# Attention of a decoder layer: one loop over heads, and an unrolled order over head pairs

## The reference, cut to what matters

```python
# MLA, 8 heads, query and key width 96, value width 64, dense causal
s = einsum('bqhd,bkhd->bhqk', qi, k) * scale
p = masked_softmax(s, kpos <= qpos)
o = einsum('bhqk,bkhd->bqhd', p, v)
# NSA, 8 heads in 2 groups that share keys and values, width 64; three branches with a relative bias
#   compressed: 63 keys; selected: all causal 64-token blocks that top-16 of 16 gives; window: the last 512 keys
out = gi[..., 0:1] * o_cmp + gi[..., 1:2] * o_slc + gi[..., 2:3] * o_win
```

## Time and profile before

| what | us |
|---|---|
| median of 3 runs | 4298.7 (4294.97 to 4320.84) |
| the profiled execution | 4301.82 |
| its span | 4300.0 |
| TensorE busy over the span | 3597.1 (84%) |
| VectorE busy | 1310.4 (30%) |
| ScalarE busy | 648.4 (15%) |
| mean granted TensorE clock | 0.822 |

### The profile page before, as it was taken

One profiled execution on the slowest core, in us unless ns is written; L12 is line 12 of the kernel. 1 busy time (PEld: TensorE's weight loads), 2 busy tenths in 40 slices (PEclk: granted clock), 3 DMA queues, 4 the chain that ended last, 5 costly groups with the idle time before them and its releaser, 6 DMA issues. The chain is left out here.

```text
span 4300.0 us, 50598 instructions
## 1 busy us (share of the span) xinstructions
PE 3597.1 (84%) x16004; PEld 2660.0 (62%) x16005; DVE 1310.4 (30%) x3711; ACT 648.4 (15%) x1506; POOL 176.3 (4%) x187
## 2 busy tenths in 40 slices
PE   3447765899999998798499999999999999999970
PEld 1124445667666666465477776877778777777750
DVE  1114551443443343355222221222222222222213
ACT  0001110232333332132101000100011000100100
POOL 0000000000000000011000000000000000000000
PEclk7678885555566655897699999999999999999995
DMA  3222223211111011221566445764677655555716
GB/s 105 94 107 42 44 35 59 48 36 36 36 35 36 23 36 30 95 62 35 199 229 220 172 155 186 261 227 172 224 261 264 220 191 207 214 175 184 263 61 234
DMA packets 345115, 571.32 MB, mean 133 GB/s; under 512 B 123134, under 2 KB 150142, under 8 KB 343912
## 3 DMA queue, kind: packets, MB, share of 16 engines
q1 hardware_dynamic: 304984, 526.53, 36.7%
q0 software_dynamic: 21152, 38.50, 2.6%
q10 hardware_dynamic: 18832, 4.33, 0.5%
HBM read 531.15 MB, written 72.19 MB: 140 GB/s over the span
## 5 line engine op out<-in xcount | busy, mean ns | idle before, releaser
L1539 PE MATMUL ps<-xT_e,wg 128*128 128x128 f32 (+2 forms) x8192 | 1266.8, 318 | 71.1 <-DVE aT L1502 50.0
L1539 PEld LDWEIGHTS ps<-xT_e,wg 128*128 128x128 f32 x8192 | 1224.9, 200 | 126.3 <-DVE aT L1502 54.0
L1550 PE MATMUL ps<-wd,aT 128*128 128x512 f32 x1504 | 650.8, 592 | 0.0
L1550 PEld LDWEIGHTS ps<-wd,aT 128*128 128x128 f32 x1504 | 283.3, 190 | 344.4 <-issue 344.4
L1495 DVE TENSOR_SCALAR gg<-ps,bias 128x128 f32<-128x128 f32 (+2 forms) x256 | 101.4, 396 | 764.5 <-PE ps L1539 764.5
L696 PE MATMUL ps<-kn,qn 64*128 64x512 f32 (+3 forms) x384 | 270.8, 841 | 0.0
L711 PE MATMUL ps<-ident_t,sc 128*128 128x128 f32 x880 | 224.5, 393 | 44.8 <-ACT sc L754 29.4
L1508 DVE COPY ys_e<-ps 128x1024 f32<-128x1024 f32 x47 | 56.1, 1221 | 671.7 <-PE ps L1550 671.7
L754 ACT ACTIVATE sc<-sc,nm 128x640 f32<-128x640 f32 (+15 forms) x256 | 164.3, 642 | 638.2 <-DVE nm L790 638.2
L711 PEld LDWEIGHTS ps<-ident_t,sc 128*128 128x128 f32 x880 | 148.4, 197 | 170.1 <-issue 166.5
L728 PEld LDWEIGHTS ps<-vn,pT 128*128 128x128 f32 x1056 | 233.5, 325 | 0.0
(11 more groups left out here) (284 smaller groups left out, 2891.8 us busy)
## 6 DMA issues: line engine op xcount, KB each, us to landing
wg<-in_w_gate_up SPq DMA_DIRECT2D x128, 2048.0 KB, 7.8
wd<-in_w_down SPq DMA_DIRECT2D x128, 1024.0 KB, 4.9
yr<-d_ys SPq DMA_DIRECT2D x8, 2048.0 KB, 7.3
skew<-d_rev SPq DMA_DIRECT2D x18, 512.0 KB, 5.2
w_in<-in_w_in SPq DMA_DIRECT2D x1, 6880.0 KB
d_strip<-strip SPq DMA_DIRECT2D x9, 512.0 KB, 2.6
x_a<-in_x POOLq DMA_DIRECT2D x8, 512.0 KB, 7.5
kn<-d_kn SPq DMA_DIRECT2D x8, 512.0 KB
```

Of the source, the lines that this page charges most:

```text
L1539: mm = pe.matmul(ps[:, j % 2, half * PASS:half * PASS + w], wg[:, j // 2, k, c0:c0 + 255:2], xT[:, k, 0:w], start=(k == 0), stop=(k == KD ...
L1550: mm = pe.matmul(ps[:, 2 + 2 * b + h, :], aT[:, j, b * P:(b + 1) * P], wd[:, c, j % 2, h * 512:(h + 1) * 512], start=(j == 0), stop=(j == ...
```

## The change

`stage_attend` is written out for pairs of heads, with no loop. A unit is a pair, a branch and a query block. 18 wide units and 14 narrow ones alternate, with m, s and w mixed, and the four last wide ones follow one another.

- The scores of the two NSA heads of a unit are formed from operands in partitions 0 to 63 and 64 to 127, into different banks. They are cut into pieces of at most 512 keys. m keeps 96 rows for each of its heads.
- VectorE's custom instruction now multiplies by -1 and takes the minimum, which gives the negative maximum itself. It is issued for each head and piece, and the second piece starts from the first one's result. L790 goes.
- ScalarE copies the transposed tiles of the first head of the pair, VectorE those of the second.
- The reciprocal, the gate product and some last products are issued once for both heads.
- Loads are double-buffered by pair, and the first two pairs' loads are issued at the start. `sc` is set to zero by GpSimd, over 8192 columns instead of 4096.
- The gates are stored as rows of 24 numbers, and not as 12-byte pieces, and are loaded once, as the last load of the first pair; VectorE waits for them in its second unit.

```diff
-                        with nc.allow_non_contiguous_dma("12-byte gates"):
-                            sp.dma_start(e.d_gt[:, rows, :].rearrange("h p d -> p h d"), gt[b][:, :].rearrange("p (h d) -> p h d", d=3)).then_inc(s_st, 16)
+                        sp.dma_start(e.d_gt[rows, :], gt[b][:, :]).then_inc(s_st, 16)
...
+    BIG = [("m", 7), ("m", 6), ("s", 7), ("m", 5), ("s", 6), ("m", 4), ("w", 7), ("s", 5), ("m", 3), ("w", 6), ("s", 4), ("w", 5), ("m", 2),
+           ("s", 3), ("w", 4), ("s", 2), ("w", 3), ("w", 2)]
+    SMALL = [("m", 1), ("m", 0), ("c", 7), ("c", 6), ("c", 5), ("c", 4), ("c", 3), ("s", 1), ("c", 2), ("w", 1), ("c", 1), ("s", 0), ("c", 0), ("w", 0)]
+    ORDER = [x for i in range(len(BIG)) for x in BIG[i:i + 1] + SMALL[i:i + 1]]
+    PAIRS = HM // 2
+    NU = len(ORDER)
+    UNITS = [(hp, b, q) for hp in range(PAIRS) for b, q in ORDER]
...
+        qm, km = sb("qm", [QK, 2, 2, S]), sb("km", [QK, 2, 2, S])
+        vm = sb("vm", [P, 2, 2, NT, VD])
+        qn = sb("qn", [P, 2, S])
+        kn = sb("kn", [P, 2, 2, S])
...
+        sc = sb("sc", [P, DEPTH, 2, S])
+        pT = sb("pT", [P, 2, 2, S])
+        nm, rs, co = sb("nm", [P, DEPTH, 2, 2]), sb("rs", [P, DEPTH, 2]), sb("co", [P, DEPTH, 2])
...
+        def pieces(u):
+            full = width(*UNITS[u][1:])
+            return [(FIRST[u] + c // 512, c, min(512, full - c)) for c in range(0, full, 512)]
+        def by_scalar(h, g):
+            return h == 0
...
+                pool.memset(sc[:, :, :, :], 0.0).then_inc(s_set, 1)
...
+                def load_mla(hp):
+                    k = hp % 2
+                    if hp >= 2:
+                        sp.wait_ge(s_y, NU * (hp - 1))
+                    sp.dma_start(qm[:, k, :, :], e.d_qm[2 * hp:2 * hp + 2].rearrange("h d n -> d h n")).then_inc(s_lm[k], 16)
+                    sp.dma_start(km[:, k, :, :], e.d_km[2 * hp:2 * hp + 2].rearrange("h d n -> d h n")).then_inc(s_lm[k], 16)
+                    for h in range(2):
+                        sp.dma_start(vm[:, k, h, :, :], e.d_vm[2 * hp + h].rearrange("(t p) d -> p t d", p=P)).then_inc(s_lm[k], 16)
+                def load_nsa(hp):
+                    k, g = hp % 2, hp // 2
+                    sp.dma_start(qn[:, k, :], e.d_qn_flat[2 * hp:2 * hp + 2].rearrange("h d n -> (h d) n")).then_inc(s_ln[k], 16)
+                    for h in range(2):
+                        half = slice(h * HD, (h + 1) * HD)
+                        sp.dma_start(kn[half, k, :, :], e.d_kn[:, g * HD:(g + 1) * HD, :].rearrange("w d n -> d w n")).then_inc(s_ln[k], 16)
+                        sp.dma_start(ck[half, k, :], e.d_ck[g]).then_inc(s_ln[k], 16)
+                        sp.dma_start(strip[:, k, h, :], e.d_strip[2 * hp + h]).then_inc(s_ln[k], 16)
+                        sp.dma_start(wstrip[:, k, h, :], e.d_wstrip[2 * hp + h]).then_inc(s_ln[k], 16)
+                        sp.dma_start(vn[:, k, h, :, :], e.d_vn[h][g].rearrange("(t p) d -> p t d", p=P)).then_inc(s_ln[k], 16)
+                    sp.dma_start(cv[:, k, :], e.d_cv[g]).then_inc(s_ln[k], 16)
+                    if hp == 0:
+                        sp.dma_start(gates[:, :, :, :], e.d_gt.rearrange("(t p) (h b) -> p t h b", p=P, b=3)).then_inc(s_gate, 16)
...
+                load_nsa(0)
+                load_mla(1)
+                load_nsa(1)
+                for hp in range(PAIRS):
+                    if hp + 2 < PAIRS:
+                        load_mla(hp + 2)
+                        load_nsa(hp + 2)
+                    store(hp)
...
+                    lo = tiles(b, q)[0] * P
+                    for piece, c0, w in pieces(u):
+                        if piece >= 2:
+                            pe.wait_ge(s_m, 2 * (piece - 1))
+                        for h in range(2):
+                            half = slice(h * HD, (h + 1) * HD)
+                            out = ps[:, 2 * (piece % 2) + h, 0:w]
+                            cols = slice(lo + c0, lo + c0 + w)
+                            rows = slice(q * P, (q + 1) * P)
+                            if b == "m":
+                                mm = pe.matmul(out, qm[:, k, h, rows], km[:, k, h, cols], start=True, stop=True)
+                            elif b == "c":
+                                mm = pe.matmul(out, qn[half, k, rows], ck[half, k, 0:w], start=True, stop=True)
                             else:
...
+                                mm = pe.matmul(out, qn[half, k, rows], kn[half, k, "sw".index(b), cols], start=True, stop=True)
+                            mm.then_inc(s_s, 1)
...
+                for u in range(len(UNITS)):
+                    turn(u, 0)
+                    if u:
+                        values(u - 1)
+                    if TURNS[u + 1] - TURNS[u] == 2:
+                        turn(u, 1)
+                    if u + 2 < len(UNITS):
+                        scores(u + 2)
+                values(len(UNITS) - 1)
...
+                def exps(u):
+                    k, n = u % DEPTH, parts(u)
+                    w = width(*UNITS[u][1:])
+                    for h in range(2):
+                        act.wait_ge(s_m, 2 * (FIRST[u + 1] - 1) + h + 1)
+                        act.activation(sc[:, k, h, 0:w], sc[:, k, h, 0:w], ACT.Exp, bias=nm[:, k, h, n - 1:n], scale=-1.0,
+                                       accum_out=rs[:, k, h:h + 1]).then_inc(s_p, 1)
...
-                        ch(dve.tensor_tensor_reduce(sc[:, i % 4, 0:w], src, bias, 1.0, -3.0e38, ALU.add, ALU.max, mx[:, i % 4:i % 4 + 1]))
-                        dve.tensor_scalar(nm[:, i % 4:i % 4 + 1], mx[:, i % 4:i % 4 + 1], -1.0, None, ALU.mult).then_inc(s_m, 1)
...
+                        dve.tensor_tensor_reduce(sc[:, k, h, c0:c0 + w], ps[:, 2 * (piece % 2) + h, 0:w], bias_of(u, h, c0, w), -1.0,
+                                                 nm[:, k, h, c - 1:c] if c else 3.0e38, ALU.add, ALU.min, nm[:, k, h, c:c + 1]).then_inc(s_m, 1)
...
+                    step(dve.reciprocal(co[:, k, :], rs[:, k, :]))
+                    O = ps[:, 6 + u % 2, 0:2 * VD].rearrange("p (h d) -> p h d", d=VD)
+                    if b != "m":
+                        i = "csw".index(b)
+                        step(dve.tensor_tensor(co[:, k, :], co[:, k, :], gates[:, q, 2 * hp:2 * hp + 2, i], ALU.mult))
+                    if SEEN[(hp, "m" if b == "m" else "n", q)] == u:
+                        dve.tensor_tensor(y[:, hp % 2, q, :, :], O, bcast(co[:, k, :].unsqueeze(2), [P, 2, VD]), ALU.mult).then_inc(s_y, 1)
+                    else:
+                        dve.scalar_tensor_tensor(y[:, hp % 2, q, 0, :], O[:, 0, :], co[:, k, 0:1], y[:, hp % 2, q, 0, :], ALU.mult, ALU.add)
+                        dve.scalar_tensor_tensor(y[:, hp % 2, q, 1, :], O[:, 1, :], co[:, k, 1:2], y[:, hp % 2, q, 1, :], ALU.mult, ALU.add).then_inc(s_y, 1)
...
+                for u in range(len(UNITS)):
+                    if u == 1:
+                        dve.wait_ge(s_gate, 16)
+                        step(dve.tensor_scalar(gates[:, 0, :, 0], gates[:, 0, :, 0], cvalid[:, 0:1], None, ALU.mult))
+                    if u + 1 < len(UNITS):
+                        peak(u + 1, 0)
+                    copies(u, 0)
+                    if u + 1 < len(UNITS):
+                        peak(u + 1, 1)
+                    if u:
+                        finish(u - 1)
+                    copies(u, 1)
+                finish(len(UNITS) - 1)
```

More of the change, by code:

```diff
@@ L604, in width, with parts @@
         return min(NCMP, (P * (q + 1) - CMP_LEN) // CMP_STRIDE + 1) if b == "c" else P * len(tiles(b, q))
[L606 to L610, removed]
+    def parts(u):
+        return (width(*UNITS[u][1:]) + 511) // 512
+    FIRST = [sum(parts(k) for k in range(u)) for u in range(len(UNITS) + 1)]
+    DEPTH = 4
@@ new lines, in turn @@
+                def turn(u, g):
+                    n = len(tiles(*UNITS[u][1:]))
+                    for h in range(2):
+                        pe.wait_ge(s_p, 2 * u + h + 1)
+                        if TURNS[u] + g:
+                            pe.wait_ge(s_cp[h], TURNS[u] + g)
+                        for i in range(4 * g, min(n, 4 * g + 4)):
+                            mm = pe.transpose(ps[:, 4 + h, (i % 4) * P:(i % 4 + 1) * P], sc[:, u % DEPTH, h, i * P:(i + 1) * P], ident[:, :])
+                        mm.then_inc(s_t[h], 1)
@@ L723, in values @@
+                def values(u):
+                    hp, b, q = UNITS[u]
+                    k = hp % 2
+                    ts = tiles(b, q)
+                    if u >= 2:
+                        pe.wait_ge(s_y, u - 1)
+                    for h in range(2):
+                        out = ps[:, 6 + u % 2, h * VD:(h + 1) * VD]
+                        pe.wait_ge(s_cp[h], TURNS[u + 1])
+                        for n, t in enumerate(ts):
                             if b == "c":
                                 w = width(b, q)
```

(22 more changed lines are left out.)

266 lines of the change are left out of this document (94 added, 172 removed).

## The result

The changed kernel takes 3851.33 us, the median of 4 runs (3836.1 to 3860.74), against 4300.05 us for the kernel before. The ratio is 0.8945, with a 95% interval of 0.8903 to 0.8987. The profiled execution has a span of 3852.9 us and a mean granted clock of 0.896.
First the windows of the attention stage, in the columns of the earlier trace rows: the loads, the start, and the last three of the four pairs, cut roughly where a pair ends.

The account below looks back on a forecast made before the run. TensorE was taken to bound the attention stage, mostly at a low clock. Start 27, pairs 440, waits 22 and clock loss 53 made 542 us in place of 959, so 3882 us for the kernel; range 3825 to 4160 us.

Parts of the forecast that it names:

- case A: Attention stage: the forecast itself, high clock with TensorE pacing, 3882 us; 3829 us if no time is lost to the clock; chance 0.46.
- B: Attention stage: clock high, but the chain over VectorE decides; 3945 us; chance 0.15.
- C: Attention stage: clock low for half of the time; stage 709 us, kernel 4049 us; chance 0.20.
- start of the stage: Before the first matmul and at the gates: 16.5 us for loading plus 10.5 us more, 27 us in all.
- four pairs at the high clock, with waits: TensorE's work in attention: 110 us for a pair, 440 us for four, plus 5% waits, 22 us.
- low clock: Attention stage: a low start and falls in narrow units, 12% of the time at half speed, 53 us.
- The halves: NSA scores on both row halves: factor 0.57, an NSA tile at the high clock 0.455 us in place of 0.55.
- The warning: Attention stage, cited for case B: tiling speeds TensorE but not the emptying of PSUM; 3945 us, chance 0.15.

Follow-up runs that it names:

- The runs with 96 and 128 rows: Kernel before, NSA queries and keys loaded again, partly or wholly, so scores run over 96 or 128 rows: 4051.58 and 3987.93 us, with changed expert routing.
- the one with one half: Changed kernel with both NSA heads' operands in partitions 0 to 63, so their scores run one after another; new order kept: 3909.68 us, ratio 0.9059.
- the old order: Changed kernel with each pair's units in order m, c, w, s, query blocks 0 to 7; pairs and halves kept: 3889.6 us, ratio 0.8999.
- the narrow units last: Changed kernel with a pair's 18 wide units first and its 14 narrow ones behind them: 3879.44 us, ratio 0.8991.
- the kernel with c last: Kernel before with a head's branches in order m, w, s, c, so the eight compressed steps stand at the end: 4094.48 us, ratio 0.9496.

## Why the prediction was right

The forecast was 3882 us, the measured time 3851.33 us, and case A held: the high clock, paced by TensorE. That the time lies in the range says little, since cases A, B and C all do; the granted clock and TensorE's missing waits decide for A, which had a chance of 0.46. Against the terms of the sum:

| term | forecast, us | measured, us |
|---|---|---|
| start of the stage | 27 | 20 to the first matmul; no price shows for the gates |
| four pairs at the high clock, with waits | 440 + 22 | 4 x 118 = 472 |
| low clock | 53 | about 7 (13 us at half speed) |
| filling and emptying the row of units | none | 2 |
| the stage | 542 | 501 |

The stage was forecast 41 us too long, and the rest of the kernel came out 11 us longer than taken, so that the whole is 30 us off. The loss to the clock is mis-sized by 46 us. The other terms miss by 7, 10 and 2 us, not all the same way, so that they nearly cancel.

- The clock. I took the high clock since the halves fill the rows that NSA scores leave idle. The runs with 96 and 128 rows speak for the rows bearing on it, and the one with one half shows that more rows weren't needed in this order. The conclusion was right, its reason half of the truth, and so in part luck. By the Trainium skill's page "TensorE: Matmul & The Clock Gate" (What's actually happening), how busy the engine was sets the clock. These runs don't bear that out for busy time: the 128-row run stays at 1.00 with TensorE busy for 35 of 41 us, and the kernel before stays at 0.50 with 77 of 77.
- A reading was wrong. I wrote that no head shows a rise in the steps of w and s. The first head does, near its end (and two others like it), while TensorE runs the last selected step's transposes and values, over 128 rows, and no scores:

```profile
872.27 1.91 PE L711 MATMUL ps<-ident_t,sc 128*128 128x128 f32 x8
873.98 4.31 PE L728 MATMUL ps<-vn,pT 128*128 128x64 f32 x30
...
876.00:877.00 1.00, 1.00 (x11) 1.00 (x11) 0.40 (x3) 0.00 (x0) 0.00 (x0) 1.00 0.00 0
```

So the MLA scores weren't needed for a rise even there, which fits the runs with more rows.

- The loss to the clock was mis-sized. I took falls in the narrow units from the earlier trace rows. In the trace the clock is low for 6 us after the first matmul and for 7 from 788 us on, and never in a narrow unit after that. Those falls belong to narrow steps that follow one another, as the runs with the old order and with the narrow units last show: 17 to 27 us for each pair.
- TensorE's work was too small in the sum, and its waits too large. A pair takes 118 us in place of 110 and 5.5 of waits. TensorE's waits are about 1 us of it, and the transposes stand out: from start to start they take 31 us of the second pair for 220 of them, 0.142 us each against 0.115. That they now come in smaller groups may be why; no run shows it.
- The halves. The factor was taken at 0.57, and is about 0.52 in a wide unit. They are worth 56 us; the forecast's terms gave 4 x 12.5 = 50 us.
- VectorE and ScalarE. 85 us forecast and 79 measured on VectorE, 71 and 61 on ScalarE. 43 us more on VectorE cost the stage 4 to 8 us, and the kernel's time doesn't tell it from nothing. The warning in the Trainium skill's page "TensorEngine Tiling (Array Packing)" (PSUM Bottleneck) did not bite: the trace has TensorE busy for 119 of 120 us in the second pair.
- Code without a loop costs nothing that shows, as costed. The rest of the kernel is 11 us longer in this profile than before, 6 of them in the expert stage, which the change doesn't touch.

What stays open is what exactly the clock goes by. The runs show two things that work on it here (rows filled, wide units beside narrow ones), and that either is nearly enough with pairs. The pairs seem to be a third: without either, the clock is high for some 230 us of the stage, against some 160 us in the kernel before. But loads ahead and fewer VectorE instructions came with them, and no run takes them apart. The runs don't show a rule that would give each fall and rise, and the three low heads of the kernel with c last were not explained.

## What to carry to other kernels

Read the granted clock by stretches before costing a stage that is bound by TensorE. A stage at 0.50 with TensorE busy all the time is worth more than any instruction that could be saved in it, and where a run of narrow steps stands can decide it: the move of eight small steps brought 5% here. Put narrow steps singly beside wide ones of other work, and use the idle rows of the array. But look at the clock again afterwards: the compressed steps spread in the old loop brought nothing. And don't count the gains of two such edits one by one: either alone had nearly all of it.

## What the hardware showed that I had not expected

- A clock that was high held through 44.6 us of one head's steps with scores over 64 rows (the kernel with c last), while the same steps, entered at the low clock, were low for 77 us.
- The same matmuls with the same columns ran at 1.00 over 128 rows where they ran at 0.50 over 64, so that a kernel whose matmuls fill more rows, and which loads more, took 258 us less in its stage.
- Between 64 and 128 rows it goes by degrees: in the second head the low stretch around the compressed steps was 27 us with 96 rows and 14 us with 128, and the stage took 754.7 and 697.9 us.
- The add with a minimum that starts from an earlier result takes 0.746 us for 512 keys, against 0.692 us when it starts from a constant.
